# Second block of a fused two-block network: how values and gates are projected, and where the compressed branch stands

## The reference, cut to what matters

```python
z = h @ w_in            # 512 x 1024 times 1024 x 2328
g_rnn, x_rnn, q, k_c, v_c, k_s, v_s, k_w, v_w, gate_logits = split(z)
rnn = gelu(g_rnn) * rg_lru(causal_depthwise_conv(x_rnn, conv_w, conv_b), ...)
kc = gelu(blocks(k_c + pos) @ cmp_w1_k) @ cmp_w2_k     # 31 blocks of 32 tokens, for each of 2 groups
vc = gelu(blocks(v_c + pos) @ cmp_w1_v) @ cmp_w2_v
gates = sigmoid(gate_logits)                           # 24 columns
# attention over kc/vc, over k_s/v_s and over k_w/v_w, each scaled by its gate and added
```

## Time and profile before

| | |
|---|---|
| median of 3 runs | 1999.46 us (1990.83 to 2000.87) |
| profiled execution | 1992.1 us, span 1990.0 us |
| TensorE | 94% of the span busy, mean granted clock 0.956 |
| ScalarE, VectorE, GpSimd | 39%, 51%, 44% busy |
| DMA | 92 GB/s over the span |

### The profile page before, as it was taken

One profiled execution on the slowest core, in us unless ns is written; L12 is line 12 of the kernel. 1 busy time (PEld: TensorE's weight loads), 2 busy tenths in 40 slices (PEclk: granted clock), 3 DMA queues, 4 the chain that ended last, 5 costly groups with the idle time before them and its releaser, 6 DMA issues. The chain is left out here.

```text
span 1990.0 us, 26010 instructions
## 1 busy us (share of the span) xinstructions
PE 1872.8 (94%) x8878; PEld 1513.5 (76%) x8878; DVE 1021.1 (51%) x1797; ACT 777.2 (39%) x1235; POOL 882.1 (44%) x1158
## 2 busy tenths in 40 slices
PE   6999999999999999999999999997887799999997
PEld 5767788888887866788888878886555588888885
DVE  6667556666654377566666555333763342222223
ACT  3444443333334344443333334554653242222223
POOL 5543445555555532454555553337001325555551
PEclk9999999999998999999999999988887879999998
DMA  6221224444322221233444321213001202322311
GB/s 232 85 85 43 75 80 145 146 143 147 131 73 97 87 83 43 87 104 136 149 137 148 105 84 66 85 43 127 1 1 43 85 0 95 116 84 86 125 42 43
DMA packets 102964, 183.46 MB, mean 92 GB/s; under 512 B 6714, under 2 KB 66668, under 8 KB 100844
## 3 DMA queue, kind: packets, MB, share of 16 engines
q1 hardware_dynamic: 102504, 181.74, 26.6%
q10 hardware_dynamic: 388, 0.79, 0.1%
HBM read 180.42 MB, written 2.10 MB: 92 GB/s over the span
## 5 line engine op out<-in xcount | busy, mean ns | idle before, releaser
L772 POOL TENSOR_TENSOR w_lo<-raw,w_hi 128x256 fp32r<-128x256 f32 (+1 forms) x1148 | 879.2, 799 | 1068.7 <-ACT w_hi L815 1068.4
L1896 PE MATMUL ps<-n_hi,w_hi 128*128 128x512 f32 x1408 | 560.9, 398 | 9.5 <-DVE n_lo L1278 5.5
L1897 PE MATMUL ps<-n_lo,w_hi 128*128 128x512 f32 x1408 | 551.8, 392 | 0.0
L1898 PE MATMUL ps<-n_hi,w_lo 128*128 128x512 f32 x1408 | 551.5, 392 | 0.0
L815 ACT ACTIVATE w_hi<-raw 128x1024 fp32r<-128x1024 f32 (+1 forms) x331 | 310.5, 944 | 322.6 <-PE ps L1898 199.3
L1896 PEld LDWEIGHTS ps<-n_hi,w_hi 128*128 128x128 f32 x1408 | 266.7, 189 | 70.3 <-issue 9.7
L1897 PEld LDWEIGHTS ps<-n_lo,w_hi 128*128 128x128 f32 x1408 | 266.4, 189 | 57.5 <-issue 3.4
L1898 PEld LDWEIGHTS ps<-n_hi,w_lo 128*128 128x128 f32 x1408 | 266.3, 189 | 56.4
L1896 PE MATMUL ps<-x_hi,w_hi 128*128 128x512 f32 x672 | 273.2, 406 | 8.9 <-DVE x_lo L1278 8.9
L1897 PE MATMUL ps<-x_lo,w_hi 128*128 128x512 f32 x672 | 269.1, 400 | 0.0
L1898 PE MATMUL ps<-x_hi,w_lo 128*128 128x512 f32 x672 | 268.8, 400 | 0.0
(11 more groups left out here) (270 smaller groups left out, 1992.2 us busy)
## 6 DMA issues: line engine op xcount, KB each, us to landing
raw<-in_w_up SPq DMA_DIRECT2D x44, 1024.0 KB, 6.9
raw<-in_w_ff SPq DMA_DIRECT2D x32, 1024.0 KB, 6.1
raw<-in_w_in SPq DMA_DIRECT2D x28, 1024.0 KB, 7.3
zb<-in_ada_w SPq DMA_DIRECT2D x16, 1536.0 KB, 8.1
raw<-in_w_down SPq DMA_DIRECT2D x44, 512.0 KB, 4.3
raw<-in_w_out SPq DMA_DIRECT2D x12, 1024.0 KB, 6.7
za<-in_x SPq DMA_DIRECT2D x1, 2048.0 KB, 10.1
raw<-in_cmp_w_k SPq DMA_DIRECT2D x2, 1024.0 KB, 6.7
```

Source lines behind the costliest of these rows:

```text
L772: last = pool.tensor_tensor(parts[0][:, c], parts[1][:, c], parts[2][:, c], ALU.subtract)
L1896: pe.matmul(out, l_hi, r_hi, start=start, stop=False)
L1897: pe.matmul(out, l_hi, r_lo, start=False, stop=False)
L1898: return pe.matmul(out, l_lo, r_hi, start=False, stop=stop)
```

## The change

Values and gates are projected as `features` does it (24 matmuls, the weight columns stationary), copied by ACT to SBUF, and turned by four transposes on TensorE into bank 7, from which ACT copies the rows to where they stood before. The compressed branch moves from behind g_rnn to between the other projections, its weight stripes with it, on every queue. Its buffers are laid elsewhere, so that it can be prepared ahead of the recurrence.

```diff
-    add(("g_rnn",), "F", 4)
     add(("cmp", 0), "C", 4)
+    add(("q2",), "F", 4)
     add(("cmp", 1), "C", 4)
+    add(("g_rnn",), "F", 4)
...
+        cval = [tiles(part[:, :, :].rearrange("p m s -> p (m s)"), 16) for part in (sq, ss)]
+        turned_in = {"vsel": zc[:, 1536:2048], "vwin": zc[:, 1024:1536], "gates": zc[0:24, 512:1024]}
...   (ACT)
+            block_hi(0)
             decay(0)
             keys(0)
+            values("vsel", STR["kvs",].g0 + 3)
             decay_root(0)
             decay(1)
             keys(1)
+            value_rows("vsel", 0)
+            decay_root(1)
+            values("vwin", STR["kw",].g0 + 1)
+            decay(2)
             ensure(STR["kw",].g0 + 3 + LOOK)
+            value_rows("vwin", 1)
+            ensure(STR["cmp", 0].g0 + 2 + LOOK)
+            decay_root(2)
+            ensure(STR["cmp", 0].g0 + 3 + LOOK)
+            act.activation(turned_in["gates"], filled(act, ("gates",))[0:24, :], ACT.Sigmoid)\
                 .then_inc(freed(("gates",)), 1)
+            decay(3)
+            ensure(STR["cmp", 0].g0 + 4 + LOOK)
+            block_hi(1)
+            block_hidden(0)
+            decay_root(3)
             queries(0)
+            block_turned(0)
             queries(1)
+            act.activation(zd[:, 1024:1120], filled(act, ("gates", "rows"))[:, 0:96], ACT.Copy)\
+                .then_inc(freed(("gates", "rows")), 1)
+            block_out(0)
             queries(2)
             queries(3)
+            ensure(STR["cmp", 1].g0 + 4 + LOOK)
+            block_hidden(1)
             act.wait_ge(rnn_ready, HT)
             (gelu of g_rnn 0 to 3; block_turned(1) behind 1, block_out(1) behind 2)
...   (DVE: both cval additions and block_lo(0) ahead of the recurrence, block_lo(1) behind it)
...   (PE)
+            def narrow(key, g, width):
+                wh, wl = quarter(g)
+                out = bank(key)
+                for k in range(DT):
+                    last = product(out[0:width, :], wh[:, k * width:(k + 1) * width], wl[:, k * width:(k + 1) * width],
+                                   n_hi[:, k, :], n_lo[:, k, :], k == 0, k == DT - 1)
+                last.then_inc(quarter_done, 1)
+            def narrow_rows(name):
+                src = turned_in[name]
+                width = src.shape[0]
+                emptied(pe, (name,))
+                out = bank((name, "rows"))
                 for t in range(NT):
+                    last = pe.transpose(out[:, t * width:(t + 1) * width], src[:, t * P:(t + 1) * P],
+                                        ident[0:width, 0:width])
+                last.then_inc(full[BK[name, "rows"][0]], 1)
...
-            tokens_narrow(("vsel",), STR["kvs",].g0 + 3, P)
+            narrow(("vsel",), STR["kvs",].g0 + 3, P)
             recurrence_gates(1)
             features([("kw",)], STR["kw",].g0)
-            tokens_narrow(("vwin",), STR["kw",].g0 + 1, P)
-            tokens_narrow(("gates",), STR["kw",].g0 + 2, 24)
+            narrow_rows("vsel")
+            narrow(("vwin",), STR["kw",].g0 + 1, P)
             recurrence_gates(2)
+            narrow(("gates",), STR["kw",].g0 + 2, 24)
+            narrow_rows("vwin")
             recurrence_gates(3)
+            block_products(0)
+            features([("q2", 0)], STR["q2",].g0)
+            narrow_rows("gates")
+            block_turn(0)
+            features([("q2", 1)], STR["q2",].g0 + 1)
+            block_results(0)
+            features([("q2", t) for t in range(2, 4)], STR["q2",].g0 + 2)
+            block_products(1)
+            features([("g_rnn", 0)], STR["g_rnn",].g0)
+            features([("g_rnn", 1)], STR["g_rnn",].g0 + 1)
+            block_turn(1)
+            features([("g_rnn", 2)], STR["g_rnn",].g0 + 2)
+            block_results(1)
+            features([("g_rnn", 3)], STR["g_rnn",].g0 + 3)
```

More of the change, by code:

```diff
@@ L141, in plan @@
     add(("kw",), "W", 3)
+    add(("cmp", 0), "C", 4)
     add(("q2",), "F", 4)
+    add(("cmp", 1), "C", 4)
     add(("g_rnn",), "F", 4)
[L144 to L145 removed]
     add(("out2", 0), "F", 4)
@@ L321, in bank_plan @@
     b.take(("gates",), 2, st["kw",].g0 + 2)
-    for name in ("q2", "g_rnn"):
-        for t in range(4):
-            b.take((name, t), t, st[name,].g0 + t)
+    for name in ("vsel", "vwin", "gates"):
+        b.take((name, "rows"), 7)
+    b.take(("chid", 0), 3, st["cmp", 0].g0 + 3)
+    for t in range(4):
+        b.take(("q2", t), t, st["q2",].g0 + t)
+    b.take(("chid", 1), 2, st["cmp", 1].g0 + 3)
+    for t in range(4):
+        b.take(("g_rnn", t), t, st["g_rnn",].g0 + t)
     for t in range(HT):
@@ L431, in build @@
         zd = sb("zd", [P, 3328])
-        tb = sb("tb", [P, 3, S])
+        with ExitStack() as part:
+            tb = sb("tb", [P, 3, S], F32, part)
+        cb_hi = sb("cb_hi", [P, 16, 64], F32R)
+        sb("rest_of_tb", [P, S])
         sq = sb("sq", [P, 2, S])
@@ L445, in build @@
         blkw = sb("blkw", [P, 2, HT, P])
-        rotF = sb("rotF", [P, 2, S])
+        with ExitStack() as part:
+            rotF = sb("rotF", [P, 2, S], F32, part)
+        cb_lo = sb("cb_lo", [P, 16, 64], F32R)
         fgw = sb("fgw", [P, DT, 2])
@@ L452, in build @@
         x_lo = sb("x_lo", [P, 4, S], F32R)
[L453 to L457, removed]
+        zy = sb("zy", [P, 4096])
         banks = ctx.enter_context(nc.psum_tensor("ps", [P, 8 * S], F32))
@@ L709, in _, with load_cmp @@
             w2 = a["w_in_2"][0]
[L710 to L713, removed]
+            def load_cmp(j, name):
                 slot = room(("cmp", j))
@@ L717, in _ @@
                 two(slot, [(r[:, 0:8], v[:, 0:8]), (r[:, 8:16], v[:, 8:16])])
+            load_f(("x_rnn",), w2[:, 512:1024])
+            load_f(("kvs",), w2[:, 1536:2048])
+            load_f(("kw",), w2[:, 2048:2328])
+            load_cmp(0, "cmp_w1_k_2")
+            load_f(("q2",), w2[:, 1024:1536])
+            load_cmp(1, "cmp_w1_v_2")
+            load_f(("g_rnn",), w2[:, 0:512])
             for j in range(2):
@@ L1078, in keys @@
             def keys(j):
-                key, vkey = ((("kvs", 2), ("vsel",)), (("kw",), ("vwin",)))[j]
                 ensure(STR["kvs",].g0 + (3, 5)[j] + LOOK)
+                key = (("kvs", 2), ("kw",))[j]
                 b = filled(act, key)
@@ L1126, in _ @@
                     .then_inc(freed(("g_rnn", t)), 1)
[L1128 to L1144, removed]
+                if t == 1:
+                    block_turned(1)
+                if t == 2:
+                    block_out(1)
             for n in range(NU + 4):
@@ L1697, in _, with block_lo @@
                 ins.then_inc(freed(("x_rnn", t)), 1)
+            for j in range(2):
+                emptied(dve, ("kvs", j))
+                v = kk[j].rearrange("p g (c j r) -> p j g c r", j=8, r=2)
+                for half in range(2):
+                    c = POS_ROW + 16 * j + 8 * half
+                    for g in range(2):
+                        last = dve.tensor_tensor(
+                            cval[j][:, 8 * half:8 * half + 8, g * NCMP:(g + 1) * NCMP],
+                            v[:, :, g, half:half + NCMP, 0],
+                            cols[:, 1, c:c + 8].unsqueeze(2).to_broadcast([P, 8, NCMP]), ALU.add)
+                last.then_inc(val_ready, 1)
+            def block_lo(j):
+                k = slice(0, 2 * NCMP)
+                split_lo(SPL["cmp",] + j, cval[j][:, :, k], cb_hi.bitcast(F32)[:, :, k], cb_lo[:, :, k])
+            dve.wait_ge(val_ready, SPL["cmp",] + 2)
+            block_lo(0)
             for t in range(HT):
@@ L1709, in _ @@
                 dve.tensor_tensor_scan(gr[:, t, :], rn[2], rn[6], 0.0, ALU.mult, ALU.add).then_inc(rnn_ready, 1)
+            block_lo(1)
             dve.wait_ge(rnn_ready, HT)
-            emptied(dve, ("gates",))
+            emptied(dve, ("gates", "rows"))
             dve.tensor_scalar(gates[:, 0, 0:HEADS2], gates[:, 0, 0:HEADS2], const[:, C_SEEN:C_SEEN + 1], None,
                               ALU.mult).then_inc(gate_set, 1)
[L1716 to L1729, removed]
             for t in range(HT):
@@ L2303, in _ @@
                 last.then_inc(full[BK["cout", j][0]], 1)
-            for key in (("kvs", 2), ("vsel",), ("kw",), ("vwin",), ("cout", 0), ("cout", 1)) \
+            block_products(0)
[12 more added lines that the diff above has]
+            features([("g_rnn", 3)], STR["g_rnn",].g0 + 3)
+            for key in (("kvs", 2), ("kw",), ("vsel", "rows"), ("vwin", "rows"), ("cout", 0), ("cout", 1)) \
                     + tuple(("q2", t) for t in range(4)):
```

49 lines of the change are left out of this document (28 added, 21 removed).

## The result

| | kernel before | changed kernel |
|---|---|---|
| median | 2000.16 us (4 runs, 1990.83 to 2003.28) | 1968.35 us (4 runs, 1964.06 to 1973.68) |
| profiled execution | 1992.1 us, span 1990.0 | 1970.72 us, span 1968.7 |
| ratio | | 0.9854, 95% interval 0.983 to 0.9879 |
| again, on another occasion | 1996.82 us (11 runs) | 1971.61 us (6 runs), ratio 0.9871 (0.9847 to 0.9895) |

A forecast was written before the change was run, and what follows sets the result against it. TensorE, busy 94% of the span, was taken as the bound. Removing 36.5 us and adding 1.5 transposes, 7.5 stalls and 2.5 clock saves 25.0: 1992.1 becomes 1967.1, put at 1970 for the runs' level, range 1956 to 1985.

The forecast's parts named there:

- Values and gates: vsel and vwin fall from 10.7 to 5.5 us each, 10.4 saved; gates from 17.3 to 5.5, 11.8 saved.
- Recurrence gates 2: They ran in the low clock too: 2.8 us to the next start against 1.4 at full clock, 1.4 us saved.
- Compressed branch: 25.9 us become 11.3 of matmuls and 1.7 of transposes and small products, stalls gone: 12.9 us saved.
- Transposes: Three times four added on TensorE, 0.5 us per four: 1.5 us in all, ends 1 and 3.
- New waits: TensorE waits for weights at the branch's third and fourth quarter, first q2, second branch's last quarter, first g_rnn: 7.5 us.
- Clock: The new stalls, shorter and split, bring one drop to half clock costing 2.5 us, ends 0 and 8.
- Sum: 36.5 - 1.5 - 7.5 - 2.5 = 25.0 us saved; the profiled execution of 1992.1 us becomes 1967.1.
- The runs' level: Two of four earlier executions lay 9 us higher, unexplained; the prediction was therefore put between, at 1970.
- Signs: Among them: attention's first score matmul 25 to 27 us earlier than 1384.55, time from there to the end unchanged.
- A: ACT's order becomes the bound, its weight copies holding TensorE: 10 us more stalls, 3 of clock, 1983 us; chance 0.14.
- B: Clock stays down from gates to end of q2: whole stretch 2005 us, chance 0.04; about half 1987 us, chance 0.08.
- C: Only turned projections pay, the moved branch is paid back in stalls: 19.6 us saved, 1972.5 up to 1976; chance 0.12.

The follow-up runs named there:

- Turned alone: The kernel before with only vsel, vwin and gates projected by 24 matmuls and turned, the compressed branch left behind g_rnn: 1968.15 us, again 1971.13 us.
- sums early: The changed kernel with the 24 one-column modulation sums put ahead of x_rnn, 8 before and 16 behind the spreads: 1967.40 us.
- sums apart: The changed kernel with 4 modulation sums in the final norm's wait, 10 behind x_rnn's first two tiles, 10 behind the third, DVE's modulation behind its convolutions: 1966.89 us.
- the experiment on the weights: The changed kernel with ACT's weight copy for the compressed branch's third quarter put ahead of decay(2): 1967.06 us.
- the move alone: The changed kernel with values and gates projected by tokens_narrow again, the compressed branch still between the projections: 1987.93 us, ratio 0.9958.
- changed, again: The changed kernel itself, nothing altered, measured once more beside the kernel before: 1971.61 us, ratio 0.9871.

## Why the prediction was right

- **Values and gates** (10.4 + 11.8 us): `vsel` and `vwin` 5.5 us each. A matmul with 24 weight columns streams like one with 128, the value I had chosen between 111 and 458 ns: from the first of the 24 to the transposes it was 5.96 us, 0.5 more than I took. Turned alone, 22.1 us were expected and 21.1 and 22.4 measured.
- **What a stream of matmuls costs**: The Trainium skill ("TensorE: Matmul & The Clock Gate", "Back-to-back issue gap") gives for a sustained stream of weight loads and matmuls about 81 ns each at 128 columns and 131 ns at 512. By that, as an estimate, turning one value projection round would save 96 x 81 - 24 x 131 ns = 4.6 us. The rows here have 111 and 229 ns and 10.7 - 5.5 = 5.2 us, so the measurement decides.
- **Recurrence gates 2** (1.4 us): length 1.88 at full clock everywhere in the changed kernel.
- **Compressed branch** (12.9 us): no product waited for `cb_hi` or `cb_lo`, and the transposes and small products ran without a stall behind full tiles.
- **Transposes** (1.5 us): a group of four has a length of 0.60 us but costs 0.36, 0.43 and 0.35 us to the next start, 1.1 us in all.
- **New waits** (7.5 us): 2.51, 2.02, 0.47 and 1.14 us, 6.1 in all (6.8 by the steps from start to start), at four of the five places named; the third quarter, named too, came in time. The recurrence's scans ended at 1281.4, 1293.3, 1307.0 and 1318.9, which less the 7.1 us of late start is 1274.3, 1286.2, 1300.0 and 1311.8, against 1274, 1286, 1299 and 1312 in the walk.
- **Clock** (2.5 us): none in one profile of the changed kernel, 2.1 us (102.0 - 99.9) in the other. With the same waits it was none for the sums early and 3.4 us at half clock for the sums apart. So 2.5 us fits one of four profiles with these waits.
- **Sum**: with the measured sizes, 36.5 - 0.5 (gates) - 1.1 - 6.8 = 28.1 us against the stage's 27.8. The second profile has 25.7, and the forecast was 25.0: low in both. The waits were taken 0.7 us too large by steps, the transposes 0.4, the gates 0.5 too small, and in the first profile the clock drop did not come.
- **The runs' level**: I had left open what lifts some executions by 9 us. A good part is the half clock that begins at the spreads ahead of x_rnn, 3.4 to 23.9 us long: 7 us between the two first profiles. Had the changed kernel's profile been read as it stands, 1992.1 - 1970.7 = 21.4 us, the stage's gain would have been taken 6 us too small.
- **Luck**: That 1970 lies within 2 us of both medians is partly luck. The profile was forecast at 1967.1 and measured 1970.7: 2.8 us more than forecast came from the stage, 0.6 from the rest, and the 7.1 us lost ahead of it were not in the sum. The 2.9 us between 1967.1 and 1970 stood for a spread of the runs that was not explained.
- **Signs**: Two of those named were missed. The first score matmul came 20.8 and 17.1 us earlier than 1384.55, not 25 to 27, because the start had slipped; and the time from there to the end, said to stay, was 605.5 us before and 604.9 and 601.7 after.
- **Rivals**: A (ACT's order as the bound) did not come, but the experiment on the weights shows that ACT's queue is what stands next: shift one step and another of the same size is late. B did not come in any profile: where `narrow` takes the gates they run at 1.00. Its case was weighed on a wrong reading, though: the trace of the kernel before has drops not only behind pauses of 2.5 us and more, but also from 1214.0 us, behind 1.19 us, and from 1384.7, behind 0.47, 0.36 and 0.85 us among small products. Its price for the half, 1987 us, does not follow from its own rule either (1970 - 2.5 + 18 = 1985.5). C, the move paid back in stalls, is refuted by the profiles (8.0 us for the move alone) and by the span at full clock (some 3 us on top of the turned projections); in the medians of the turned and the changed kernel what is left does not show.

## What to carry to other kernels

Count a projection by instructions and by what the weight load costs. For few output columns, let the few be stationary and stream the long side, then turn the result round; here 10.7 us became 5.5 + 0.6. A piece with very little work per instruction can cost twice: under the 24-column matmuls the clock fell to half, under the 128-column ones it stayed at full, and so the gates were 1% of the arithmetic of the stage and 17 of its 128 us. Before comparing two profiles, line them up at the start of the changed stage; what lies ahead of it may differ by 7 to 9 us without any change there. And multiply each run's span by its mean clock: that showed a gain of 3 us that the medians hid.

## What the runs showed of the hardware that was not expected

- The clock can stay down under steady work. At the spreads of the norms it fell to half (1.2 GHz) in every profile, behind a wait of 1.19 us and also where sums filled that wait. With three one-column sums behind each pair of x_rnn's products it was back after 3.4 us in four profiles, ahead of the first product, and after 20.5 to 23.9 us in four others, at the same place and with the same instructions; with pure products there it was 10.2 us in each of four profiles, and 6.8 + 3.4 in a fifth. That the sums hold it down is likely by this, not shown.
- The fall behind a short wait is not certain either. Four profiles have the same waits of 2.5 and 1.8 to 2.1 us within 6 us: the clock stayed at 1.00 in two (changed, sums early) and stood at half for 3.4 us (sums apart) and 6.8 us (changed, again) in the others.
- Matmuls of 24 columns that follow each other without a pause, the weight load busy throughout, brought the clock down within their first 6 us in all four profiles that have them, and it stood at half for 13.7 to 23.9 us; 96 matmuls of 128 columns, with the same 111 ns a step, did not.
- One DVE subtraction of 128x992 elements took 5.37 us in one execution and 1.2 to 1.7 us in the others looked at; no run here says why.
